# Nearly all up panels of three perceptrons with seven products each, in two sets of blocks and banks

## The reference, cut to what matters

```
h = h + square(relu(rms_norm(h) @ ff_w1)) @ ff_w2        # FF: 1024 -> 4096 -> 1024
x = layer_norm(ALPHA * x + (silu(x @ w_gate) * (x @ w_up)) @ w_down)   # GLU0, GLU1: 1024 -> 2816 -> 1024
```

## Time and profile before

| | us |
|---|---|
| median of 3 runs (lowest, highest) | 1963.46 (1961.86, 1964.05) |
| the profiled execution | 1964.29 |
| its span, first to last instruction | 1962.5 |

### The profile page before, as it was taken

One profiled execution on the slowest core, in us unless ns is written; L12 is line 12 of the kernel. 1 busy time (PEld: TensorE's weight loads), 2 busy tenths in 40 slices (PEclk: granted clock), 3 DMA queues, 4 the chain that ended last, 5 costly groups with the idle time before them and its releaser, 6 DMA issues.

```text
span 1962.5 us, 29944 instructions
## 1 busy us (share of the span) xinstructions
PE 1928.8 (98%) x12504; PEld 1281.4 (65%) x12504; DVE 1124.7 (57%) x1547; ACT 810.1 (41%) x1313; POOL 339.4 (17%) x355
## 2 busy tenths in 40 slices
PE   8999999999999999999999999999999999999997
PEld 5655655657676654886567666648766586666576
DVE  6666786656477642245767765523565668656224
ACT  6443411445355531133545544312464545444222
POOL 1011111410034320024011511100500124211001
PEclk9999999999999999999999999999999999999999
DMA  7211200232312322322230323323111123232321
GB/s 251 86 65 65 79 29 22 86 129 87 129 64 87 126 99 99 108 108 87 68 120 30 129 87 129 108 93 144 44 65 47 41 86 108 87 129 87 121 94 44
DMA packets 28241, 179.83 MB, mean 92 GB/s; under 512 B 2961, under 2 KB 7185, under 8 KB 7185
## 3 DMA queue, kind: packets, MB, share of 16 engines
q1 hardware_dynamic: 27312, 170.93, 24.5%
q10 hardware_dynamic: 512, 4.94, 0.7%
q0 software_dynamic: 288, 2.10, 0.3%
HBM read 175.86 MB, written 2.10 MB: 91 GB/s over the span
## 4 chain that ended last, share of the span: by engine, by line
PE 67%; DVE 1%; ACT 1%; issue 0%; ACTq 0%; DVEq 0%
PE psum_a L422 17%; PE psum_a L424 17%; PE psum_a L423 17%; PE psum_b L422 4%; PE psum_b L424 4%; PE psum_b L423 4%; PE psum_b L559 2%; PE psum_b L1171 1%; PE psum_a L1125 0%; PE psum_a L1190 0%; PE psum_b L570 0%; PE psum_a L1238 0%; PE psum_a L1245 0%; PE psum_den L1171 0%; PE psum_b L850 0%; PE psum_b L722 0%
## 5 line engine op out<-in xcount | busy, mean ns | idle before, releaser
L2015 DVE SCALAR_TENSOR_TENSOR W_PARTS<-W,W_PARTS 128x2048 f16<-128x2048 f32 x111 | 255.2, 2301 | 306.3 <-ACT W_PARTS L1346 306.2
L1346 ACT ACTIVATE W_PARTS<-W 128x2048 f16<-128x2048 f32 x111 | 211.0, 1904 | 275.0 <-PE psum_a L424 272.7
L422 PE MATMUL psum_a<-U,W_PARTS 128*128 128x512 f16 (+1 forms) x808 | 301.6, 373 | 1.5 <-DVE U L2135 1.5
L423 PE MATMUL psum_a<-U,W_PARTS 128*128 128x512 f16 (+1 forms) x808 | 301.4, 373 | 0.0
L424 PE MATMUL psum_a<-U,W_PARTS 128*128 128x512 f16 (+1 forms) x808 | 301.4, 373 | 0.0
L422 PE MATMUL psum_a<-ARENA,W_PARTS 128*128 128x256 f16 (+1 forms) x860 | 269.1, 313 | 2.3 <-DVE ARENA L2668 2.3
L424 PE MATMUL psum_a<-ARENA,W_PARTS 128*128 128x256 f16 (+1 forms) x860 | 269.0, 313 | 0.0
L423 PE MATMUL psum_a<-ARENA,W_PARTS 128*128 128x256 f16 (+1 forms) x860 | 268.9, 313 | 0.0
L2975 POOL TENSOR_TENSOR ARENA<-ARENA 128x512 f16<-128x512 f32 x76 | 108.0, 1431 | 430.8 <-ACT ARENA L1480 430.7
L424 PEld LDWEIGHTS psum_a<-U,W_PARTS 128*128 128x128 f16 x808 | 79.1, 98 | 90.4
L422 PEld LDWEIGHTS psum_a<-U,W_PARTS 128*128 128x128 f16 x808 | 79.1, 98 | 87.7 <-issue 4.1
(11 more groups left out here) (376 smaller groups left out, 4044.7 us busy)
## 6 DMA issues: line engine op xcount, KB each, us to landing
W<-weights SPq DMA_DIRECT2D x159, 1024.0 KB, 4.8
CON<-const ACTq DMA_DIRECT2D x1, 3071.5 KB, 12.9
X<-x_in SPq DMA_DIRECT2D x4, 256.0 KB, 4.0
X<-x_in SPq DMA_DIRECT2D x1, 1024.0 KB, 8.0
U<-dft POOLq DMA_DIRECT2D x1, 1024.0 KB, 5.8
ARENA<-dft POOLq DMA_DIRECT2D x1, 1024.0 KB, 5.4
U<-mem_in ACTq DMA_DIRECT2D x1, 1024.0 KB, 4.8
y_out<-U SPq DMA_DIRECT2D x2, 512.0 KB, 2.9
```

The costliest lines, as they stand in the source:

```text
L422: nc.tensor.matmul(out, left(0), right(0), start=first, stop=False, skip_group_check=goes_on)
L423: nc.tensor.matmul(out, left(0), right(1), start=False, stop=False, skip_group_check=goes_on)
L1346: nc.scalar.activation(HOMES[home_of[g]][:, 0, :], W[g % 2][:, :], ACT.Copy, scale=W_SCALE).then_inc(sem("panel_high"), 1)
L2015: nc.vector.scalar_tensor_tensor(out=home[:, 1, :], in0=W[g % 2][:, :], scalar=W_SCALE, in1=home[:, 0, :], op0=ALU.mult, op1=ALU.subtract) ...
```

## The change

**Panels.** Only one plain panel is left after the two at the start of each perceptron: FF has up 2 plain and up 3 to 15 with seven products (13), a GLU gate 1 plain and then up 1, gate 2, up 2, ..., gate 10, up 10 with seven products (19). The host lays out their weights by blocks.

**Two sets.** Panels with an even number in this list use the old place for the blocks and `psum_b`; odd ones use `ODD_BLOCKS`, the first 3584 of the 4096 float32 columns of `W_PARTS`, and `psum_den` with two banks of `psum_a`. So q7 of the panel before is run between q5 and q2 of the present one, and its q4 between q6 and q3. A down panel's split waits for the last odd panel's q4, since its home is `W_PARTS`.

**Orders.** ScalarE and VectorE have new loops, one pass per panel; `rest_high` opens ScalarE's pass, and the last finish and last hidden copy of the panel before end it. Gate tiles now come from seven products too: their parts are added to `TS`, and `gate_silu` applies silu to them in three pieces. A semaphore of GpSimd's zeroed tile (`at_zeroed`) is merged with its neighbour (`mla_kr_ready`).

The diff, cut to its core:

```diff
-        PART = [SQ[:, n, :] for n in range(3)]
+        PART = lambda at, i: SQ[:, 3 if i == 1 and at % 2 else i, :]
+        ODD_BLOCKS = block_parts(W_PARTS[:, :, :].rearrange("p a b -> p (a b)")[:, 0:7 * BLOCK])
...
-                if gated:
-                    self.pairs = [(("gate", j), ("up", j)) for j in range(1, groups)]
-                else:
-                    self.pairs = [(("up", j), ("up", j + 1)) for j in range(2, groups, 2)]
-                self.seven = {b: seven_before + n for n, (_, b) in enumerate(self.pairs)}
+                self.plain, self.sevens = (("gate", 1), [("up", 1)]) if gated else (("up", 2), [])
+                for j in range(2 if gated else 3, groups):
+                    self.sevens += [("gate", j), ("up", j)] if gated else [("up", j)]
...
+        seven_order = []
+        for M in (FF, GLU0, GLU1):
+            for at, key in enumerate(M.sevens):
+                n = M.seven[key]
+                earlier_one = at > 0
+                for name in ("q1", "q5", "q7", "q2", "q6", "q4", "q3"):
+                    if name not in ("q7", "q4"):
+                        seven_order.append((n, name))
+                    elif earlier_one:
+                        seven_order.append((n - 1, name))
+            seven_order += [(n, "q7"), (n, "q4")]
+        seven_at = {one: i + 1 for i, one in enumerate(seven_order)}
...
+                def sixth(at):
+
+                    key = M.sevens[at]
+                    pe.wait_ge(sem("panel_low"), panel_of[(M.name,) + key] + 1)
+                    pe.wait_ge(sem("part_read"), 3 * M.seven[key] + 3)
+                    pe.wait_ge(sem("v_low"), 4 * MLPS[M.norm] + 3)
+                    one_of_seven(at, "q7")
+
+                def seventh(at):
+
+                    pe.wait_ge(sem("tile_added"), 3 * M.seven[M.sevens[at]] + 3)
+                    pe.wait_ge(sem("v_low"), 4 * MLPS[M.norm] + 4)
+                    one_of_seven(at, "q4")
+
+                def seven_panel(at):
+
+                    key = M.sevens[at]
                     n, g = M.seven[key], len(released)
                     panel_of[(M.name,) + key] = g
                     home_of.append(IN_BLOCKS)
-                    earlier.append(None)
-                    released.append((sem("seven_done"), 7 * n + 7))
+                    earlier.append((last_in.get(0), last_in.get(1)) if at == 1 else None)
+                    released.append((sem("seven_done"), seven_at[n, "q4"]))
+                    if at % 2:
+                        last_in[0] = last_in[1] = g
                     pe.wait_ge(sem("blocks_low"), 2 * n + 1)
-                    if n:
-                        pe.wait_ge(sem("tile_21"), n)
-                    one_of_seven("q1")
+                    if at > 1:
+                        pe.wait_ge(*last_read(M, at - 2))
+                    one_of_seven(at, "q1")
                     pe.wait_ge(sem("blocks_low"), 2 * n + 2)
                     pe.wait_ge(sem("v_low"), 4 * MLPS[M.norm] + 1)
-                    if n:
-                        pe.wait_ge(sem("tile_added"), 3 * n - 1)
-                    one_of_seven("q5")
-                    one_of_seven("q2")
+                    if at > 1:
+                        pe.wait_ge(sem("tile_added"), 3 * (n - 2) + 2)
+                    elif at == 1:
+                        for freed, uses in spare:
+                            pe.wait_ge(freed, uses)
+                    one_of_seven(at, "q5")
+                    if at:
+                        sixth(at - 1)
+                    one_of_seven(at, "q2")
                     pe.wait_ge(sem("part_read"), 3 * n + 1)
                     pe.wait_ge(sem("v_low"), 4 * MLPS[M.norm] + 2)
-                    one_of_seven("q6")
+                    one_of_seven(at, "q6")
+                    if at:
+                        seventh(at - 1)
                     pe.wait_ge(sem("part_read"), 3 * n + 2)
-                    one_of_seven("q3")
-
-                def sixth(key):
-
-                    pe.wait_ge(sem("panel_low"), panel_of[(M.name,) + key] + 1)
-                    pe.wait_ge(sem("part_read"), 3 * M.seven[key] + 3)
-                    pe.wait_ge(sem("v_low"), 4 * MLPS[M.norm] + 3)
-                    one_of_seven("q7")
-
-                def seventh(key):
-
-                    pe.wait_ge(sem("tile_added"), 3 * M.seven[key] + 3)
-                    pe.wait_ge(sem("v_low"), 4 * MLPS[M.norm] + 4)
-                    one_of_seven("q4")
+                    one_of_seven(at, "q3")
...
+                spare = [(A.free[(A.n + i) % 4], (A.n + i) // 4) for i in range(2)]
+                seven_banks = (psum_b, [psum_den] + [A.banks[(A.n + i) % 4] for i in range(2)])
+                for at in range(len(M.sevens)):
+                    seven_panel(at)
+                before = len(M.sevens) - 1
+                pe.wait_ge(sem("tile_added"), 3 * M.seven[M.sevens[before]])
+                pe.wait_ge(*last_read(M, before - 1))
...
             def raw_high(M, key):
 
                 n, g = M.seven[key], panel_of[(M.name,) + key]
                 act.wait_ge(landed[g % 2], 16 * (g // 2 + 1))
-                if n:
-                    seven_done(act, n - 1, "q3")
-                nc.scalar.activation(M.blocks[:, 0, A11:A12 + 1].rearrange("p b k c -> p (b k c)"), W[g % 2][:, 0:2 * BLOCK], ACT.Copy, scale=W_SCALE)\
+                if M.sevens.index(key) > 1:
+                    seven_done(act, n - 2, "q3")
+                elif M.sevens.index(key) == 1:
+                    for home in earlier[g]:
+                        act.wait_ge(*released[home])
+                elif n:
+                    seven_done(act, n - 1, "q4")
...
+            def gate_silu(M, key, part):
+
+                n, j, at = M.seven[key], key[1], M.sevens.index(key)
+                tile = TS[:, 2 * (j % 2) + (part > 0)]
+                if part < 2:
+                    act.wait_ge(sem("tile_added"), 3 * n + 2 + part)
+                    src = tile = tile if part == 0 else tile[:, HALVES[1]]
+                    nc.scalar.activation(tile, src, ACT.Silu).then_inc(sem("gate_ready"), 1)
+                else:
+                    seven_done(act, n, "q4")
+                    if j >= 3:
+                        act.wait_ge(*last_read(M, 2 * j - 6))
+                    nc.scalar.activation(tile[:, HALVES[0]], banks_of(M, at)[0][:, 0:HALF], ACT.Silu, scale=-DESCALE).then_inc(sem("gate_ready"), 1)
...
+                def finished(at, m):
+
+                    key = M.sevens[at]
+                    if not M.gated:
+                        if m:
+                            tile_21(M, key)
+                        hidden_high(M, key[1], (m,))
+                    elif key[0] == "up":
+                        hidden_high(M, key[1], (m,))
+                    elif m == 0:
+                        gate_silu(M, key, 0)
                     else:
-                        rest_high(M, seven)
-                        plain_tile(M, plain, 0)
-                        split(panel_of[(M.name,) + seven] + 1)
-                        plain_tile(M, plain, 1)
-                        for i in range(3):
-                            read_part(M, seven, i)
-                        v_high(M, (V7, V4))
-                        for j in range(1 if M.gated else 2):
-                            hidden_high(M, j)
-                    if before and not M.gated:
-                        hidden_high(M, plain[1])
-                    before = seven
-                split(panel_of[(M.name,) + before] + 2)
-                hidden_high(M, before[1], (0,))
-                if not M.gated:
-                    tile_21(M, before)
-                hidden_high(M, before[1], (1,))
+                        gate_silu(M, key, 1)
+                        gate_silu(M, key, 2)
+
+                for at in range(1, len(M.sevens)):
+                    key = M.sevens[at]
+                    rest_high(M, key)
+                    read_part(M, key, 0)
+                    read_part(M, key, 1)
+                    if at + 1 < len(M.sevens):
+                        raw_high(M, M.sevens[at + 1])
+                        sums_high(M, M.sevens[at + 1])
+                    if at == 1 and not M.gated:
+                        hidden_high(M, M.plain[1])
+                    if M.gated:
+                        finished(at - 1, 0)
+                        read_part(M, key, 2)
+                        finished(at - 1, 1)
+                    else:
+                        read_part(M, key, 2)
+                        tile_21(M, M.sevens[at - 1])
+                        hidden_high(M, M.sevens[at - 1][1])
+                last = len(M.sevens) - 1
+                down = panel_of[(M.name,) + M.sevens[last]] + 1
+                split(down)
+                split(down + 1)
+                finished(last, 0)
+                finished(last, 1)
...
+                if n:
+                    dve.wait_ge(sem("blocks_low"), 2 * n)
...
+                raw_low(M, first)
```

(51 more changed lines are left out.)

224 lines of the change are left out of this document (102 added, 122 removed).

## The result

The changed kernel takes 2014.91 us (median of 4 runs, 2013.08 to 2017.83) against 1963.76 us, a ratio of 1.026 (95% interval 1.024 to 1.028): slower, by 51 us where 36 were forecast. Its profiled execution took 2013.08 us, 48.8 more than that of before.

The account below looks back on a forecast made before the run. TensorE bound the kernel before, and VectorE's longer pass would bound it after: 1964.29 + 27.6 (FF) + 8.2 (both GLUs) = 2000.1 us profiled, 1999 against the median. Range 1966 to 2009; the forecast's own 1986 to 2008.

Parts of the forecast that it names:

- What bounds, and the saved products: Up parts: TensorE bounds the kernel before; 24 more seven-product panels take 28.2 us off it if supply keeps up.
- FF's pass: FF, per panel: VectorE's closed loop through ScalarE takes 10.2 us, 11.4 with GpSimd, over TensorE's 9.18.
- FF put together: FF, first product to down part: 27.6 us longer, from slower passes, a later start and a new wait at the end.
- The meetings: GpSimd's subtractions beside VectorE: +0.96 and +0.23 us per FF pass; bounds 0 to 1.15 per subtraction, 1969 at 0.
- Each GLU: Each GLU: two panels take 19.1 us against TensorE's 18.35 and 19.53 before; with start and tail, +4.1 us.
- rival (d): Starts and tails: TensorE's clock falls to 1.2 GHz after new waits, some 3 us each time, about 2010; chance 0.08.
- The tails: Before the first down panels: TensorE waits for the split held up by W_PARTS, 4.8 us in FF, 3.45 per GLU.
- (a): Whole kernel: order and new waits hidden, VectorE's free 30% carries everything; 1936, up to 1955; chance 0.12.
- (b): Whole kernel: the loop exists but GpSimd meets VectorE rarely; 1969, span 1961 to 1985; chance 0.22.

Follow-up runs that it names:

- rest_memset: Changed kernel with ScalarE writing the next panel's last blocks before the hidden copy, and GpSimd writing zeros where it subtracted the hidden low part: 1975.52 us.
- relief3: Changed kernel with edits of home and swap_rest, FF's squares on ScalarE, all hidden low parts on VectorE instead of GpSimd, and starts reordered: 1952.11 us.
- pool_memset: Changed kernel with GpSimd writing zeros where it subtracted, leaving out the hidden tiles' low part; waits and order stay: 1985.51 us.
- swap_rest: Changed kernel with last blocks first on ScalarE and, in the GLUs, VectorE's product reading q4's bank (L2217) ahead of sums_low: 1994.29 us.
- home: Changed kernel with each perceptron's first down panel's parts in SMALL, split during the last seven-product panel: 2004.92 us.

## Why the prediction was right or wrong

**What bounds, and the saved products**: right. Where nothing waits (rest_memset, relief3) TensorE is busy throughout, and relief3 keeps 11.7 of the 28.2 us.

**FF's pass**: right. 11.27 us for 11.4; the closed loop without GpSimd 10.19 for 10.2; the last finish at 1.65; rest_low lengthened by 0.13 where 0.23 were said.

**FF put together**: right, +26.6 for +27.6. The start's new waits sum to 8.3 us (0.64, 0.18, 2.55 and 4.96; 10 forecast), the tail's is 4.89 (4.8).

**The meetings**: right in kind. Their full worth is 29 us in the medians, and 30 were said (1999 against 1969), but that they agree so well is partly luck. With none, in the trace of pool_memset, FF is at +13.3 us from the first product to the first down matmul for +12.6, and the GLUs are at +2.3 and +1.7 for -3.6: there the forecast was too low even without GpSimd. The Trainium skill (SBUF — State Buffer, "Who interferes with whom") states that a VectorE instruction with two SBUF inputs contends with a GpSimd instruction that reads SBUF and not with one that only writes it, and calls the shared port pair an exclusive lock. The traces agree: 0.96 to 0.97 us beside a subtraction, nothing beside a write of zeros. Only the sum that I made by that rule, the full price for every subtraction (12.5), does not hold, because one of them ran in VectorE's idle time.

**Each GLU**: wrong, and it is the step that failed: +11.3 and +11.4 instead of +4.1 each, 14.5 us in the two. FF was 1.0 us below its forecast, so the profiled execution took 2013.08 for 2000.1; the medians are 2014.91 and 1999, as the profiled execution was this time below its median and not above it. "Sum 19.1, against 18.35 for TensorE" counted VectorE and ScalarE alone, and "below zero it cannot go, since VectorE sets them" took the second set of banks to be free of waits. It left out that the first product of every second panel writes the bank which VectorE's L2217 reads last in its pass, behind sums_low and a finish that meets GpSimd (1.38 for 0.42). So the binding loop closes over both engines: from a panel's first product to the addition behind its q3, 9.37 us on TensorE, and from there over L2217 to the first product two panels on, 10.06 us on VectorE; 19.43 in all. The loop that I had was priced rightly: VectorE's idle 0.35 us ahead of that addition is all the room that it has, 19.42 - 0.35 = 19.07 for 19.05.

Term by term, in the first GLU: the third panel's q1 comes 23.0 us after the first product for 21.4 (+1.6, the wait of 5.82 us for that bank). The eight loops take 1288.51 - 1130.62 = 157.9 us for 152.4 (+5.5): 0.37 us in each of them, and 2.5 more in the first, of which 1.7 are TensorE's slow clock behind that wait and 0.8 a rest_low that meets GpSimd (2.00 us at 1142.07). The tail adds 0.1. In the second GLU the first loop has no such meeting but 2.6 us of slow clock. So of the 14.5 us some 9 are the bank's and 4.3 the clock's, which is rival (d); 0.8 are the meeting's. swap_rest shows that the wait for that bank is the cause of the 0.92 us and of part of the 5.82; the share of the clock is read from the rows above, and no run takes it away alone.

**The tails**: right, 4.89, 3.44 and 3.45 us for 4.8 and 3.45; home takes them away, for part of their worth.

**Rivals (a) and (b)**: false. Even without a meeting FF's loop is 10.19 us, over TensorE's 9.18, and the last finish met GpSimd in eleven of FF's twelve passes (1.64 to 1.65).

**Rival (d), the clock**: in good part true, on top of the forecast and not in its place. It was to cost about 3 us at each tail and start. FF's tail gives 2.7, the first GLU's 0.8 and the second's nothing; FF's start gives nothing, those of the GLUs 1.7 and 2.6: some 8 us in all, where (d) had 11 (2010 against 1999). I gave it 0.08 as a case by itself and nothing in the sum.

**Range**: 1966 to 2009 was cut from the rivals as they stood: the price of a meeting below, the clock above. That a loop might exist which I had not written down, or the clock's price come on top of the meetings', had no room in it.

## What to carry to other kernels

When a cheaper product needs more help from other engines, write down every closed loop, also those through a bank: who reads it last, where that stands in its engine's order, and who writes it next. An idle gap of an engine may shelter another's use of a shared port, so removing the gap alone can return less than half of it (0.55 of 1.31 us here). A slow TensorE clock costs only where the path runs over TensorE: nothing at FF's start, which VectorE paces; up to 2.7 us at a tail, where nothing else is late; and up to 2.6 us at a start whose loop closes over TensorE. Filling a gap tests this only if the added work does not itself hold back what follows.

## What was not expected of the hardware

Two gaps of TensorE equal to 0.01 us (3.44 and 3.45) were followed by granted clocks of 0.64 and 1.00; two shorter ones differ in the same way, 2.57 us in home with 0.60 behind it and 2.55 in the kernel after with 1.00. A VectorE instruction of two SBUF inputs that meets a GpSimd subtraction is longer by 0.96 to 0.97 us whichever it is (FF's finish 1.65 for 0.68, the GLUs' 1.38 for 0.42, block sum 1.64 for 0.68), by 0.48 when the subtraction is cut in two, while a write of zeros runs inside a VectorE instruction and neither gets longer (0.52 and 1.75). What stays open is what an undisturbed clock is worth at the starts of the GLUs, and how much of the 5.1 to 6.3 us at relief3's starts another order would give back; no run settles either.
